# A gated delta rule inside a one-core two-block layer: triangular inverses by 64-blocks on quarters of TensorE, and norms folded into per-token factors

## The reference

```python
q, k, v = split(silu(causal_dwconv(qkv, conv_w)))         # 4 taps
q = l2norm(q) * 128**-0.5;  k = l2norm(k)                  # x * rsqrt(sum(x*x) + EPS)
beta = sigmoid(b_logit);  g = -exp(a_log) * softplus(a_logit + dt_bias)
# per chunk, gc = cumsum(g), dec[i, j] = exp(gc[i] - gc[j]) for i >= j
A = strict_lower(k k^T * dec * beta[:, None])
W, U0 = solve(I + A, [k * beta * exp(gc), v * beta])       # unit lower triangular
U = U0 - W S;  O = (q * exp(gc)) S + (q k^T * dec) U
S = exp(gc[-1]) * S + (k * exp(gc[-1] - gc))^T U
O = rmsnorm(O, o_gain) * silu(og)                          # over the 128 of a head
return O @ w_out
```

## Time and profile before

| | us |
|---|---|
| median of 3 runs | 2955.58 (2955.1 to 2957.2) |
| the profiled execution | 2951.39 |
| its span, first to last instruction | 2949.3 |
| the delta stage, from the rates panel to the last "do" panel | 1857.7 to 2483.8 |

### The profile page before, as it was taken

How to read it: one execution, slowest core, us unless ns; L and a number is a source line. 1 busy time by engine, 2 the same in 40 slices (tenths; PEclk the granted TensorE clock), 3 DMA queues, 4 the chain that set the end, 5 groups by cost and what they waited for, 6 DMA issues and landing times.

```text
span 2949.3 us, 43447 instructions
## 1 busy us (share of the span) xinstructions
PE 2667.0 (90%) x18436; PEld 2411.5 (82%) x18436; DVE 1420.1 (48%) x2126; ACT 1038.8 (35%) x1658; POOL 1073.4 (36%) x660
## 2 busy tenths in 40 slices
PE   6999877799999899999799999799899897999997
PEld 4877766678887777778799999798899787999996
DVE  3545547463534543443572735664533334735453
ACT  4233433332323434343432323453333333333232
POOL 0643325544444121213444444201222323444444
PEclk8999988899999999999899999898999697999998
DMA  7432210333333111111122322221110001222221
GB/s 198 135 93 68 63 51 2 106 93 93 96 96 88 44 44 37 46 34 52 57 87 85 89 84 80 64 72 44 29 30 23 4 29 47 66 86 87 86 83 61
DMA packets 379921, 201.34 MB, mean 68 GB/s; under 512 B 6465, under 2 KB 377153, under 8 KB 379729
## 3 DMA queue, kind: packets, MB, share of 16 engines
q1 hardware_dynamic: 379728, 198.57, 23.7%
HBM read 196.45 MB, written 2.10 MB: 67 GB/s over the span
## 4 chain that ended last, share of the span: by engine, by line
PE 57%; DVE 22%; ACT 12%; issue 6%; POOL 2%; DMA 1%; POOLq 0%; ACTq 0%; DVEq 0%; SPq 0%
PE ps L566 39%; DVE t_ffy L2598 7%; ACT t_wh L536 4%; DVE t_ffy L2601 2%; ACT t_ffy L2517 2%; DVE t_atq L2428 2%; PE ps L2807 2%; PE ps L2245 1%; DVE t_ffy L2607 1%; PE ps L2829 1%; PE ps L419 1%; PE ps L2218 1%; PE ps L2184 1%; PE ps L964 1%; PE ps L406 1%
## 5 line engine op out<-in xcount | busy, mean ns | idle before, releaser
L546 POOL TENSOR_TENSOR t_wl<-t_raw,t_wh 128x1024 fp32r<-128x1024 f32 (+1 forms) x245 | 574.4, 2345 | 864.2 <-ACT t_wh L536 864.2
L536 ACT ACTIVATE t_wh<-t_raw 128x1024 fp32r<-128x1024 f32 (+2 forms) x327 | 332.2, 1016 | 613.9 <-PE ps L566 586.4
L566 PE MATMUL ps<-t_hh,t_wh 128*128 128x264 f32 (+2 forms) x2096 | 502.1, 319 | 32.7 <-DVE t_hl L2579 24.9
L566 PE MATMUL ps<-t_hl,t_wh 128*128 128x264 f32 (+2 forms) x2096 | 467.5, 303 | 0.0
L566 PE MATMUL ps<-t_hh,t_wl 128*128 128x264 f32 (+2 forms) x2096 | 466.3, 302 | 0.9 <-POOL t_wl L546 0.4
L566 PEld LDWEIGHTS ps<-t_hh,t_wh 128*128 128x128 f32 x2096 | 337.4, 196 | 59.7 <-issue 27.0
L566 PEld LDWEIGHTS ps<-t_hh,t_wl 128*128 128x128 f32 x2096 | 337.8, 195 | 13.2 <-issue 3.3
L566 PEld LDWEIGHTS ps<-t_hl,t_wh 128*128 128x128 f32 x2096 | 338.8, 195 | 10.9 <-issue 4.2
L566 PE MATMUL ps<-t_fhh,t_wh 128*128 128x264 f32 (+1 forms) x1056 | 287.4, 326 | 17.4 <-DVE t_fhl L2579 10.8
L566 PE MATMUL ps<-t_fhl,t_wh 128*128 128x264 f32 (+1 forms) x1056 | 286.8, 326 | 0.0
L566 PE MATMUL ps<-t_fhh,t_wl 128*128 128x264 f32 (+1 forms) x1056 | 284.1, 323 | 1.4 <-POOL t_wl L546 1.1
(11 more groups left out here) (504 smaller groups left out, 4720.5 us busy)
## 6 DMA issues: line engine op xcount, KB each, us to landing
t_raw<-in_up SPq DMA_DIRECT2D x44, 512.0 KB, 3.9
t_raw<-in_up2a SPq DMA_DIRECT2D x44, 512.0 KB, 3.9
t_raw<-in_up2b SPq DMA_DIRECT2D x44, 512.0 KB, 3.9
t_raw<-in_attn_in SPq DMA_DIRECT2D x33, 512.0 KB, 4.1
t_raw<-in_dn_in SPq DMA_DIRECT2D x33, 512.0 KB, 4.1
t_raw<-in_ada_w SPq DMA_DIRECT2D x32, 512.0 KB, 4.3
t_raw<-in_w_in SPq DMA_DIRECT2D x25, 512.0 KB, 5.0
t_raw<-in_down SPq DMA_DIRECT2D x16, 512.0 KB, 3.9
```

What stands on the lines that cost most here:

```text
L536: ac.activation(wh[j % NSPLIT][:, 0:kc, :], raw[r % NRAW][:, 0:kc, :], ACT.Copy).then_inc(up("wh_cut", "cut", j), 1)
L546: eng.tensor_tensor(wl[j % NSPLIT][:, 0:kc, :], raw[r % NRAW][:, 0:kc, :], wh[j % NSPLIT][:, 0:kc, :].bitcast(F), SUB).then_inc(up(name, " ...
L566: ins = pe.matmul(ps[2 * (j % 2) + i][:, 0:tn], wt[slot][:, k, :], a[:, k, t0:t0 + tn], start=first, stop=last)
```

## The change

Inverses: a chunk of 128 is now two diagonal blocks of 64, both worked at once in the same instructions of VectorE and as separate 64x64 matmuls whose operands and results lie on partitions 0 to 63 or 64 to 127, thus on two quarters of the array. Six levels on tiles of 64 columns per head are left (`small`). Both T and its transpose TT are kept by products: level x masks the result of `uf` (not A) and `ug` makes the two updates, one for T and one for TT. Two new steps, `uy` and `uz`, join the blocks: they make the off-diagonal 64x64 block of the transposed inverse, and ScalarE lays it out with the diagonal ones in `TF`. No transposes of T, no masking of A and no GpSimd work are left in the levels; the mask of the decays is folded into `ua` (`LEV_CAP`).

Norms: k and q stay unnormalised. The sums of squares per token go into `nsum`; `knorm` makes sqrt(sum k^2) (`nk`), beta / sum k^2 (`bt`) and an epsilon for q (`nq`) once per head group. v is multiplied by `nk`, A and the solve use `bt`, and q's norm goes into the output norm (`fs`), whose roots are taken for all heads of a group together (`froot`) and which VectorE applies straight from PSUM.

Order: the taps of a convolution of heads 4 to 7 and its silu are spread over ticks (`beside`); units start when `knorm` of their group is placed, two panels after the last q, k, v panel of the group (before: four); `finish(0)` joins the side work during the "og" panels; `finish(1)` and what is left of group 1 are drained before the "do" panels of group 1. `wl` of "og" and "do" panels moves from VectorE to GpSimd.

```diff
-LEVELS = [1, 2, 4, 8, 16, 32, 64]
+LEVELS = [1, 2, 4, 8, 16, 32]
-        LATE = ("up1", "down1", "gate", "pair", "sig", "ao", "up2", "down2", "up3", "down3")
+        LATE = ("up1", "down1", "gate", "pair", "sig", "ao", "up2", "down2", "og", "do", "up3", "down3")
         def tick():
+            if beside:
+                beside.popleft()()
...
+        def size_of(n):
+            return 64 if n else NM
         def unit(G, n):
...
-            put("ud", *u, banks=1)
-            lv = levels_of(n)
-            for x in lv[1:]:
-                put("ue", *u, x)
-                yield 1
-                put("uf" if x == lv[1] else "uft", *u, x, banks=1 if x == lv[1] else 2)
+            for x in levels_of(n):
+                put("uf", *u, x, banks=1)
                 yield 1
                 put("ug", *u, x, banks=1)
-            yield 1
+                yield 1
+            if n:
+                put("uy", *u, banks=1)
+                yield 1
+                put("uz", *u, banks=1)
+                yield 1
...
         gemm(("rate", "qkv"), lead_qkv, keep=0, feed=feed_of(2))
-        behind.extend([worker(0), worker(1)])
+        first_end = finish(0)
+        behind.extend([worker(0), worker(1), first_end])
...
-        run_first(finish(0))
+        while first_end in behind:
+            tick()
         gemm(("do",), None, every=2, group=0)
-        run_first(finish(1))
+        behind.append(finish(1))
+        drain()
...
             def uf(G, n, x):        # tensor
                 for e in range(4):
+                    for k in u.blocks:
+                        ins = pe.matmul(u.S4(b)[k, e, :], u.B("AT")[k, e, k],
+                                        u.small("T")[k, e, :] if x else lev[k, LEV_ID:LEV_ID + u.size], start=True,
+                                        stop=True)
             def ug(G, n, x):        # tensor, x > 0
+                    for e in range(4):
+                        for k in u.blocks:
+                            pe.matmul(u.half_of(b, 0, x)[k, e], u.small("TT")[k, e, :], u.cuts("Y", 0, x)[k, e],
+                                      start=True, stop=True)
+                    for e in range(4):
+                        for k in u.blocks:
+                            ins = pe.matmul(u.half_of(b, 1, x)[k, e], u.small("Y")[k, e, :], u.cuts("TT", 1, x)[k, e],
+                                            start=True, stop=True)
...
             def uf(G, n, x):        # vector
+                dv.tensor_tensor(u.small("Y"), u.S4(bank("uf", G, n, x)[0]), u.level(x),
+                                 MUL).then_inc(up("scaled", "uf", G, n, x), 1)
             def ug(G, n, x):        # vector, x > 0
+                dv.tensor_tensor(u.cuts("T", 0, x), u.cuts("T", 0, x), u.half_of(b, 0, x),
+                                 SUB).then_inc(up("scaled", "ug", G, n, x, "t"), 1)
+                dv.tensor_tensor(u.cuts("TT", 1, x), u.cuts("TT", 1, x), u.half_of(b, 1, x),
+                                 SUB).then_inc(up("scaled", "ug", G, n, x, "tt"), 1)
```

More of the change, by code:

```diff
@@ L1961, in then_qkv @@
             put("dconv", h, x)
+            rest = [lambda i=i: tap(h, x, i) for i in (1, 2, 3)] + [lambda: silu_of(h, x)]
+            if panels[j].group:
+                beside.extend(rest)
+            else:
+                for f in rest:
+                    f()
             if x == 2:
-                put("dsilu", h)
-                put_off(j, "l2_later", h, 0)
+                put_off(j, "l2_sums", h, banks=1)
         def lead_qkv(j, m):
@@ L2062, in finish @@
                 yield 1
-        def run_first(g):
-            behind.insert(0, g)
-            while g in behind:
-                tick()
         put("lev_load")
@@ L2655, in __init__ @@
                 self.qv = dq[:, self.h4, self.sl]
+                self.size = size_of(n)
+                self.blocks = [slice(a, a + self.size) for a in range(0, self.tn, self.size)]
                 self.last = levels_of(n)[-1]
-                self.second = levels_of(n)[1]
                 self.before = unit_before[G, n]
@@ new lines, in fsum @@
+            def fsum(G, e):
+                b, = bank("fsum", G, e)
+                held(b)
+                w.wait_ge(s.squared, at("squared", "fsq", G, e))
+                for n, (t0, tn) in enumerate(TILES):
+                    ins = pe.matmul(ps[b][0:tn, n:n + 1], fin[e % 3][:, t0:t0 + tn], C("ones", 128, 1), start=True,
+                                    stop=True)
+                ins.then_inc(up("summed", "fsum", G, e), 1)
+                free[b] = [(s.scaled, at("scaled", "fsum", G, e))]
@@ new lines, in fmul @@
+            def fmul(G, e):
+                w.wait_ge(s.inverted, at("inverted", "froot", G))
+                for b, tiles in zip(bank("fmul", G, e), (range(3), range(3, 5))):
+                    held(b)
+                    a0 = TILES[tiles[0]][0]
+                    for n in tiles:
+                        t0, tn = TILES[n]
+                        ins = pe.matmul(ps[b][:, t0 - a0:t0 - a0 + tn],
+                                        fs[0:tn, G, n, e:e + 1].to_broadcast([tn, 128]), C("ident", tn, tn), start=True,
+                                        stop=True)
+                    free[b] = [(s.normed, at("normed", "fmul", G, e))]
+                ins.then_inc(up("spread", "fmul", G, e), 1)
@@ new lines, in ug, with uy @@
+                ins.then_inc(up("multiplied", "ug", G, n, x), 1)
+                free[b] = [(s.scaled, at("scaled", "ug", G, n, x, "tt"))]
+            def uy(G, n):
+                u = unit_at(G, n)
+                b, = bank("uy", G, n)
+                held(b)
+                w.wait_ge(s.scaled, at("scaled", "ug", G, n, u.last, "t"))
+                for e in range(4):
+                    ins = pe.matmul(u.S4(b)[64:128, e, :], u.B("AT")[0:64, e, 64:128], u.small("T")[0:64, e, :], start=True,
+                                    stop=True)
+                ins.then_inc(up("multiplied", "uy", G, n), 1)
+                free[b] = [(s.copied, at("copied", "uy", G, n))]
@@ new lines, in uz @@
+            def uz(G, n):
+                u = unit_at(G, n)
+                b, = bank("uz", G, n)
+                held(b)
+                w.wait_ge(s.copied, at("copied", "uy", G, n))
+                w.wait_ge(s.scaled, at("scaled", "ug", G, n, u.last, "tt"))
+                for e in range(4):
+                    ins = pe.matmul(u.S4(b)[0:64, e, :], u.small("Y")[64:128, e, :], u.small("TT")[64:128, e, :],
+                                    start=True, stop=True)
+                ins.then_inc(up("multiplied", "uz", G, n), 1)
+                free[b] = [(s.copied, at("copied", "uz", G, n))]
```

466 lines of the change are left out of this document (218 added, 248 removed).

## The result

2912.93 us (median of 4 runs, 2900.08 to 2913.43) against 2956.39 for the kernel before (median of 4, 2955.1 to 2958.7): ratio 0.9842, 95% interval 0.9814 to 0.987. The profiled execution is the lowest of the four, 2900.08, while the other three took 2912.54 to 2913.43; against the profiled one of before (2951.39) it is 51.3 us less, and the medians are 43.5 apart.

What follows compares the result with a forecast made beforehand. TensorE was taken as the bound: instruction count plus waits under panels, cross-engine chains in two uncovered stretches. Stage terms summed to -39 us on the profiled 2951.4, giving 2912, and 2916 as median; range 2870 to 2955.

Steps and rivals of the forecast that it cites:

- the 18 covered panels: Delta-stage panels with units beside them, up to the end of "og": 243 us counted plus 42 lost, 285 us.
- Quarters at 0.029: Inverse's `uf` and `ug`: each 64x64 matmul on array quarters costs 0.029 us, 272 of them 7.9 us per unit.
- Rival 1: Inverse: quarters do not overlap as halves with short operands do, 0.06 us per instruction, +67 us, 2983; chance 0.10.
- A visit at 0.33: Inverse steps between panel pieces: each change of array shape costs TensorE 0.33 us, 14 per unit, 4.6 us.
- So in TensorE's count only the norms gain: TensorE's work: the inverse stays 13.5 us per unit; removing norm spreading for eight heads saves 21 us.
- Lost time 58 to 42 in the covered stretch: Panels with units beside them: time lost to waits and low clock falls from 58 to 42 us.
- rival 3: Waits nearly vanish: 20 us lost instead of 42 under panels, 54 instead of 66 at the end, 2882; chance 0.18.
- `wl` behind a step: VectorE in the covered stretch: a step of the inverse can sit behind a `wl` of 1.3 us.
- The rest of `finish(0)` and 3 steps: 8 us, where 60.7 stood: This is the gain: Gap before "do" of group 0: uncovered work shrinks from 60.7 to 8 us, named as the gain.
- The end alone, 66: Uncovered end of group 1, with chunk 4 beside nobody: 66 us, where 38.7 stood.
- rival 4: Drain only moved: chunk 4 alone runs at 1.2 GHz, +24 us, last "do" panels wait on GpSimd, +5; 2945; chance 0.07.
- "Do" of group 1, +1: Last projection panels: GpSimd makes `wl` beside an add, 2.5 us per panel of 2.9, hidden; +1 us.

Runs made afterwards that it cites:

- experiment 3: Changed kernel with the low parts (`wl`) of the output-gate and projection panels made by VectorE again instead of GpSimd: 2911.62 us, ratio 0.9841.
- the first kernel of experiment 1: Changed kernel with `finish(0)` taken out of the output-gate panels' side work and run after them, before group 0's output projection, no panel beside it: 2879.88 us, ratio 0.9751.
- experiment 2: Changed kernel with the three VectorE taps and silu of each convolution of heads 4 to 7 placed at once, not one per tick: 2937.57 us, ratio 0.9928.

## Why the time was right, and which steps were not

The 2916 forecast stands beside 2912.93, but it is partly a sum of errors that cancel, and the step that it called the gain is not the gain. The price of quarters and fewer lost us in the covered panels hold in direction; that the time came within 3 us is luck. Stage by stage the sum has the 18 covered panels 20 us too dear, and the panels before them and the end alone together 13 too cheap. In trace time its end lies 12 us too late (2447 against 2435.4; 2912 against 2900.08 for the execution), and the rest of the agreement comes from the profiled execution's being 13 us below its median, where 4 were assumed.

- *Quarters at 0.029*: right as a mean, by spacing and by doubling. Rival 1 falls. The Trainium skill (TensorE: Matmul & The Clock Gate, Part 3, "What overlaps and what doesn't") would have a load overlap a running matmul only where the row group differs; the instructions of one 64-block all share it here. By that rule the streamed columns would add to the load's time; but one quarter needs 0.058 us per instruction with 32 streamed columns (`ug`) and with 64 (`uf`, `uy`) alike. The trace does not agree.
- *A visit at 0.33*: too dear; 0.22. Over 14 visits and 8 units that is 12 us. The inverse is 7.9 + 1.0 + 14 x 0.22 = 12.0 us per unit against 13.4, not "no change".
- *"So in TensorE's count only the norms gain", -21*: the count is right, the time is not. With the instructions back the median does not move (-2.4), and most of the profile's 14 are a clock that fell in one panel. Panel 15, up to which the forecast had 7 us of gain, starts 1.7 earlier than before. They lay in part where the stage then waits for ScalarE and VectorE.
- *Lost time 58 to 42 in the covered stretch*: right direction, mis-sized. 264.6 us less the 243 counted leave 22 lost, or 29 with visits at 0.22: as in rival 3, which had 20. Its largest part had no term of its own: the taps alone are 24.6 us, in the profiles about half waits and half the clock. In the old order, with the taps in a row among other things, the new arithmetic keeps 7 us. "`wl` behind a step" was feared for nothing.
- *"The rest of `finish(0)` and 3 steps: 8 us, where 60.7 stood: This is the gain"*: this step failed. The 8 us came as forecast; that the join pays is refuted twice (+6 us in the kernel before, 33 us to be had by undoing it in the changed one). Uncovered steps were counted, 42 and 40; what they cost depends on who stands beside them. Three chains beside each other take 1.06 us per step at full clock (32.9 for 31), chunk 4 with next to nobody 1.9 at a mean clock of 0.69.
- *The end alone, 66*: 73.8. A level is 3.96 us, where the sum had 2.9 and 2 us more for all six. That is rival 4's mechanism at a third of its price. The 2.9 is right at full clock (2.98 with a filling product); what was mis-sized is the clock.
- *"Do" of group 1, +1*: 1.1 us less (24.0 to 22.9). `wl` on GpSimd is hidden, and on VectorE nearly so (22.5 us at full clock in experiment 3; 21.4, also at full clock, in the first kernel of experiment 1).

The single edits do not add up: taps 24.6, start 8.5, low parts 0 and the join -33 make 0, the whole order 36. Each is worth something else depending on whether chunk 4 is left for the end; with `finish(0)` alone, taps, start and low parts together bring 69 (2948.66 to 2879.88). How these 69 are shared among the three was not run. What the norm's other work (roots on ScalarE, multiplications on VectorE) was worth stays open too: only TensorE's part was put back.

What the orders differ by is in good part the clock. The mean granted clock of every run is on record: 0.934 to 0.939 in the changed kernel, 0.944 to 0.946 with `finish(0)` alone, 0.921 to 0.927 in the old order. With levels of 1.2 and 2.4 GHz that is some 380, 317 and 440 us at the lower one (medians). Half of a difference is what the clock can have cost where TensorE was the bound, so by this estimate up to 31 of the 33 us gained and up to 30 of the 36 lost.

## What to carry to other kernels

Count not only how many steps of side work run uncovered, but how many independent chains stand beside each other when they do: nearly the same count, 41 and 40, was some 30 us apart. A wait of TensorE can be paid twice, once as itself and once in the clock that falls after it (experiment 2; it is not so each time, as from 2091.6 to 2107.8 the changed kernel's TensorE idled 2.5 us of 16.2 at a clock of 1.00), so a row of 2 us on an evacuating engine is worth cutting into single steps even where that engine is half idle. Removed TensorE instructions are worth their time only where nothing else is waited for next; put dummies back to see.

## What the runs showed of the hardware

One panel of the same plan, with the same instructions and no idle time, ran at two clocks. In the changed kernel and in that of experiment 3:

```profile
2123.70:2136.40 12.70, 12.70 (x163) 11.71 (x163) 7.53 (x16) 3.62 (x7) 0.00 (x0) 1.00 0.17 43
```

```profile
2129.90:2148.20 18.30, 18.30 (x162) 16.75 (x163) 7.58 (x16) 3.62 (x7) 0.00 (x0) 0.64 0.12 30
```

In the panel ahead of each TensorE idled 0.8 of 16 us, so nothing in these rows tells why the one clock fell and the other did not; 5.6 us hang on whether the clock is at 2.4 or 1.2 GHz in it. The changed kernel's 12 to 13 us between its lowest run and the other three can be this: by their mean clocks (0.939, and 0.934 to 0.935) the three had 24 to 30 us more at the lower level, worth 12 to 15 us at most by the same estimate as above. In which stretches is not shown, as only the lowest was profiled. Nor is this confined to the stage that was changed: the last product ahead of the delta stage starts at 1857.6 in the profile of the changed kernel and at up to 1867.7 in those of its variants, none of which edits anything ahead of that stage. Differences under some 10 us between versions should be read with that in mind.

Two 64x64 blocks on quarters of one diagonal take 0.029 us per instruction on average (0.058 on each quarter, side by side), loads of 64 columns included, whether 32 or 64 columns are streamed. A full-array product amid them costs 0.44 us, as much as 15 of them.
